# Retention in a hybrid S5/retention block: outputs with tokens on the rows, squares summed by ScalarE, products grouped by kind, loads issued one per step

## The reference, cut to what matters

```python
h   = rms_norm(x, norm_pre)                   # x: 1024 tokens x 2048
P   = h @ W_in                                # u_s | z_s | q | k | v | z_r | gl_s | gl_r
y_s = s5_mixer(u_s) * silu(z_s)
y_r = retention(q, k, v) * silu(z_r)          # 8 heads, q/k 64 wide, v 128 wide
m   = sigmoid(gl_s) * (y_s @ W_s) + sigmoid(gl_r) * (y_r @ W_r)
x   = x + rms_norm(m @ W_out, norm_post)

# retention, per head: rotary q, k; for each chunk of tokens
inner = ((q @ k.T) * decay) @ v
cross = (q * xi) @ state                      # the state before the chunk
state = state * chunk_decay + (k * zeta).T @ v
o     = inner + cross
o     = o * rsqrt(mean(o * o over the head's 128) + eps)
```

## Time and profile before

| | |
|---|---|
| median of 3 runs | 2518.59 us (2516.74 to 2531.87) |
| the profiled execution | 2524.69 us, span 2522.9 us |
| mean granted TensorE clock | 0.962 of 2.4 GHz |
| busy, PE / DVE / ACT / POOL | 2332.7 / 1853.4 / 1150.8 / 85.2 us |
| moved by DMA | 508.67 MB, mean 202 GB/s |

### The profile page before, as it was taken

How to read it: one execution, slowest core, us unless ns; L and a number is a source line. 1 busy time by engine, 2 the same in 40 slices (tenths; PEclk the granted TensorE clock), 3 DMA queues, 4 the chain that set the end, 5 groups by cost and what they waited for, 6 DMA issues and landing times.

```text
span 2522.9 us, 28579 instructions
## 1 busy us (share of the span) xinstructions
PE 2332.7 (92%) x10288; PEld 1892.8 (75%) x10288; DVE 1853.4 (73%) x2968; ACT 1150.8 (46%) x1814; POOL 85.2 (3%) x99
## 2 busy tenths in 40 slices
PE   7898999998999999988989996989999999799994
PEld 3676778787888888886777774767887777578883
DVE  6857992977898886626887754777678988767676
ACT  4343443456555554553445443334555444245552
POOL 0000000000000000000000000440000000000000
PEclk9999997999999999999999997899999999999997
DMA  7678456765456473769555767255656655855546
GB/s 271 217 232 253 133 171 217 262 209 197 120 183 211 145 244 111 256 199 296 180 184 157 280 187 255 68 201 175 212 196 210 224 185 180 291 200 189 182 130 254
DMA packets 287888, 508.67 MB, mean 202 GB/s; under 512 B 53201, under 2 KB 69601, under 8 KB 285569
## 3 DMA queue, kind: packets, MB, share of 16 engines
q1 hardware_dynamic: 242672, 430.00, 52.1%
q10 hardware_dynamic: 36560, 46.27, 5.3%
q0 software_dynamic: 8512, 30.56, 3.7%
HBM read 394.54 MB, written 112.20 MB: 201 GB/s over the span
## 4 chain that ended last, share of the span: by engine, by line
PE 67%; DVE 16%; DMA 6%; issue 4%; ACT 3%; SPq 3%; ACTq 1%; POOL 0%; DVEq 0%; POOLq 0%
PE psum L1473 16%; PE psum L1474 16%; PE psum L1475 16%; PE psum L1469 4%; PE psum L1471 4%; PE psum L1470 4%; DMA araw<-aops 4%; DVE a_lo L1085 3%; DVE b_lo L1087 3%; PE psum L1580 1%; PE psum L1578 1%; ACT a_hi L643 1%; DVE keep L1095 1%; PE psum L1529 1%; DMA aops<-work 1%
## 5 line engine op out<-in xcount | busy, mean ns | idle before, releaser
L643 ACT ACTIVATE a_hi<-araw 128x512 fp32r<-128x512 f32 x756 | 476.5, 630 | 1197.5 <-PE psum L1475 760.8
L1473 PE MATMUL psum<-a_hi,b_hi 128*128 128x512 f32 x2352 | 930.9, 396 | 97.8 <-DVE b_lo L1087 90.7
L1474 PE MATMUL psum<-a_hi,b_lo 128*128 128x512 f32 x2352 | 923.7, 393 | 0.0
L1475 PE MATMUL psum<-a_lo,b_hi 128*128 128x512 f32 x2352 | 922.8, 392 | 0.0
L1085 DVE TENSOR_TENSOR a_lo<-araw,a_hi 128x512 fp32r<-128x512 f32 x756 | 520.9, 689 | 535.5 <-ACT a_hi L643 534.1
L1473 PEld LDWEIGHTS psum<-a_hi,b_hi 128*128 128x128 f32 x2352 | 446.6, 190 | 213.5 <-DVE b_lo L1087 107.7
L1475 PEld LDWEIGHTS psum<-a_lo,b_hi 128*128 128x128 f32 x2352 | 446.5, 190 | 94.5
L1474 PEld LDWEIGHTS psum<-a_hi,b_lo 128*128 128x128 f32 x2352 | 446.8, 190 | 91.6
L1469 PE MATMUL psum<-b_hi,a_hi 128*128 128x512 f32 x672 | 268.4, 399 | 30.2 <-DVE b_lo L1087 29.6
L1087 DVE TENSOR_TENSOR b_lo<-bx,b_hi 128x512 fp32r<-128x512 f32 x432 | 295.5, 684 | 0.0
L653 ACT ACTIVATE b_hi<-bx 128x512 fp32r<-128x512 f32 x432 | 266.5, 617 | 0.5 <-DMA bx<-in_wstream 0.2
(11 more groups left out here) (147 smaller groups left out, 1618.8 us busy)
## 6 DMA issues: line engine op xcount, KB each, us to landing
araw<-aops SPq DMA_DIRECT2D x744, 256.0 KB, 2.7
bz<-in_wstream SPq DMA_DIRECT2D x216, 256.0 KB, 3.7
bx<-in_wstream SPq DMA_DIRECT2D x116, 256.0 KB, 4.7
aops<-work SPq DMA_DIRECT2D x28, 1024.0 KB, 5.7
spill<-keep ACTq DMA_DIRECT2D x28, 1024.0 KB, 5.8
by<-in_wstream SPq DMA_DIRECT2D x108, 256.0 KB, 5.5
work<-spill SPq DMA_DIRECT2D x20, 1024.0 KB, 7.6
aops<-work POOLq DMA_DIRECT2D x15, 1024.0 KB, 5.4
```

What stands on the lines that cost most here:

```text
L643: A.activation(a_hi[:, r, :], araw[:, s % A_RING, :], ACT.Copy).then_inc(head, 1)
L1473: T.matmul(bank, b_hi[:, r, cols], a_hi[:, r, :], start=first, stop=False, skip_group_check=on)
L1474: T.matmul(bank, b_lo[:, r, cols], a_hi[:, r, :], start=False, stop=False, skip_group_check=on)
L1475: done = T.matmul(bank, b_hi[:, r, cols], a_lo[:, r, :], start=False, stop=last, skip_group_check=on)
```

## The change

1. o is computed with tokens on the partitions: the decayed scores are the stationary operand and v the moving one. All 8 products with v come first, then the 8 with the state. The squares of a head then lie along the row: ACT sums them with its accumulator, 8 calls of 128 x 128 per block. Root and reciprocal are on 128 x 8. ACT scales half of the heads (4 calls of 128 x 128), DVE the other half, PE transposes all 8 back, and DVE multiplies by z_r from PSUM. The products with ones and GpSimd's arithmetic go. The last block makes no new state.
2. Block 0's scores are made before GGR0's step 53 and decayed at its step 55, in the side banks 6 and 7. PE enters retention without a wait for ACT, and waits for ACT's last evacuation only before the first transpose of k. The last block's transposes stand before GGR1's step 3, its gating at DVE's step 5.
3. The q and k loads are issued one per step at GGR0's steps 18 to 49, v in 8 parts at every fourth step from 20 to 48, the tables at step 17 behind the waits. `load_zr` moves to GpSimd's queue.
4. y_r is loaded back at GGR1's steps 16, 19, 22 and 25, and summed at 34 to 37.
5. `load_b11` no longer loads weight tiles 4 to 7 ahead of a group that has 4.

```diff
@@ SP @@
+            def load_qk(n):
+                part, a, par, two = n // 16, n // 4 % 4, n // 2 % 2, n % 2
...
+            def load_v(n):
+                sp.dma_start(v_row[:, n, :], vrows[n]).then_inc(qkv_loaded, 16)
...
-                        load_b11(g4 + 1, k4)
+                        if k4 < TILES[g4 + 1]:
+                            load_b11(g4 + 1, k4)
...
-                if g == GGR0 and at == 44:
+                if g == GGR0 and at == 17:
                     sp.wait_ge(ys_stored, 7 * 16)
                     for b in range(4):
                         sp.wait_ge(kept_stored[b], store_until(GQK, b))
-                    load_qkv()
-                    load_zr(0)
-                    load_zr(1)
-                if g == GGR1 and at == 4:
-                    for n in range(2, 8):
-                        load_zr(n)
-                if g == GGR1 and at == 8:
...
+                    load_tables()
+                if g == GGR0 and 18 <= at < 50:
+                    load_qk(at - 18)
+                if g == GGR0 and 20 <= at < 52 and at % 4 == 0:
+                    load_v((at - 20) // 4)
+                if g == GGR1 and at in (16, 19, 22, 25):
+                    n = (at - 16) // 3
...
@@ GpSimd @@
+            load_zr(0)
+            load_zr(1)
             for n in range(BLOCKS):
-                    pool.tensor_tensor(o_t[n % 2][:, par], o_t[n % 2][:, par], o_sq[:, par], ALU.mult).then_inc(o_scaled, 1)
...
                 pool.wait_ge(z_scaled, 2 * n + 2)
...
+                if n + 2 < BLOCKS:
+                    load_zr(n + 2)
@@ ACT, retain, per block n @@
+                        A.activation(o_n[:, par], psum[:, 4 + par, :].rearrange("p (a n) -> p a n", a=4), ACT.Copy
+                                     ).then_inc(o_copied, 1)
+                    for hd in range(HEADS):
+                        act.wait_ge(o_copied, 2 * n + hd // 4 + 1)
+                        A.activation(o_junk[:, 8 * (n % 2) + hd, :], o_n[:, hd // 4, hd % 4, :], ACT.Square,
+                                     accum_out=o_sum[:, n % 2, hd:hd + 1]).then_inc(o_squared, 1)
...
+                    A.activation(o_rstd[:, n % 2, :], o_sum[:, n % 2, :], ACT.Sqrt, scale=1.0 / V_HEAD, bias=eps_sb[:, 0:1]
+                                 ).then_inc(ostd_ready, 1)
+                    act.wait_ge(o_inverse, n + 1)
+                    for a in range(4):
+                        last = A.activation(o_n[:, 0, a, :], o_n[:, 0, a, :], ACT.Copy, scale=o_rstd[:, n % 2, a:a + 1])
+                    last.then_inc(o_scaled_act, 1)
@@ DVE @@
+            def next_state(n):
+                dve.wait_ge(kv_full, n + 1)
+                dve.wait_ge(o_full, 2 * n + 2)
...
+            def scale_o(n):
+                dve.wait_ge(ostd_ready, n + 1)
+                V.reciprocal(o_rstd[:, n % 2, :], o_rstd[:, n % 2, :]).then_inc(o_inverse, 1)
+                dve.wait_ge(o_inverse, n + 1)
+                V.tensor_tensor(o_t[n % 2][:, 1], o_t[n % 2][:, 1],
+                                o_rstd[:, n % 2, 4:8].unsqueeze(2).broadcast_to([P, 4, V_HEAD]), ALU.mult).then_inc(o_scaled_dve, 1)
+            def gate_o(n):
+                dve.wait_ge(o_turned, n + 1)
...
+                for par in range(2):
+                    V.tensor_tensor(yr_ring[:, n % 2, par::2, :], psum[:, 2 + par, :].rearrange("p (a n) -> p a n", a=4),
+                                    zr_ring[:, n % 2, par::2, :], ALU.mult).then_inc(z_scaled, 1)
+            def retain():
+                for n in range(BLOCKS):
+                    if n + 1 < BLOCKS:
+                        scale_q(n + 1)
+                        decay_scores(n + 1)
+                        if n == 0:
+                            scale_k(0)
+                        next_state(n)
+                        if n + 2 < BLOCKS:
+                            scale_k(n + 1)
                     if n:
+                        gate_o(n - 1)
+                    scale_o(n)
@@ PE, retain, per block n, and the step loop @@
+                    pe.wait_ge(scores_decayed, 2 * n + 2)
+                    if n:
+                        pe.wait_ge(o_copied, 2 * n)
+                            T.matmul(psum[:, 4 + par, 128 * a:128 * a + 128], s_dec[:, par, 128 * a:128 * a + 128],
+                                     v_row[:, n, V_HEAD * hd:V_HEAD * hd + V_HEAD], start=(a == 0), stop=False,
+                                     skip_group_check=True)
+                    if n == 0:
+                        pe.wait_ge(act_evac, 4 * GGR1)
+                        turn_k(0)
+                    pe.wait_ge(q_xi_ready, n + 1)
                     if n:
+                        pe.wait_ge(state_ready, 4 * n)
+                            last = T.matmul(psum[:, 4 + par, 128 * a:128 * a + 128], q_xi[rows, a, :], ret_state[rows, a, :],
+                                            start=False, stop=(a == 3), skip_group_check=True)
                     if n + 1 < BLOCKS:
                         scores(n + 1)
+                        pe.wait_ge(k_zeta_ready, n + 1)
...
+                    if n + 2 < BLOCKS:
+                        turn_k(n + 1)
+                    if n:
+                        turn_o(n - 1)
...
+                if s == BASE[GGR0] + 53:
+                    pe.wait_ge(dve_evac, 3 * GGR0 + 3)
+                    pe.wait_ge(qkv_loaded, 40 * 16)
+                    scores(0)
                 if s == BASE[GGR1]:
                     retain()
+                if s == BASE[GGR1] + 3:
+                    turn_o(BLOCKS - 1)
                 multiply(s)
```

More of the change, by code:

```diff
@@ L409, in load_zs, with load_tables @@
                              spill[1, i, 4 * c:4 * c + 4].rearrange("k p m -> p k m")).then_inc(zs_loaded[n % 2], 16)
[L411 to L427, removed]
+            def load_qk(n):
+                part, a, par, two = n // 16, n // 4 % 4, n // 2 % 2, n % 2
+                dst = k_t if part else q_t
+                row = 32 * (2 * (a % 2) + par)
+                src = spill[4, :, 4 * part + 2 * two + a // 2, row:row + 32, :].rearrange("i p m -> p i m")
+                rows = slice(64 * par + 32 * two, 64 * par + 32 * two + 32)
+                sp.dma_start(dst[rows, a, :].rearrange("p (i m) -> p i m", i=2), src).then_inc(qkv_loaded, 16)
+            def load_v(n):
+                sp.dma_start(v_row[:, n, :], vrows[n]).then_inc(qkv_loaded, 16)
+            def load_tables():
                 sp.dma_start(area(16384, 1024), dmat).then_inc(tables_loaded, 16)
@@ L666, in free @@
                     act.wait_ge(yr_stored[1], 4 * 32)
+                if g == GGR1 and b == 1:
+                    act.wait_ge(o_turned, 8)
                 if stored(g - 1):
@@ new lines, in gate_o @@
+            def gate_o(n):
+                dve.wait_ge(o_turned, n + 1)
+                dve.wait_ge(zr_loaded[n % 2], 16 * (n // 2 + 1))
+                if n >= 2:
+                    dve.wait_ge(yr_stored[n % 2], 32 * (n // 2))
+                else:
+                    dve.wait_ge(kept_stored[0], store_until(GGR0, 0))
+                for par in range(2):
+                    V.tensor_tensor(yr_ring[:, n % 2, par::2, :], psum[:, 2 + par, :].rearrange("p (a n) -> p a n", a=4),
+                                    zr_ring[:, n % 2, par::2, :], ALU.mult).then_inc(z_scaled, 1)
@@ L1532, in outputs, with scores @@
                 pe.wait_ge(gelu_done, 8)
+            def scores(n):
+                tok = slice(BLOCK * n, BLOCK * n + BLOCK)
+                if n:
+                    pe.wait_ge(scores_decayed, 2 * n)
+                for a in range(4):
+                    for par in range(2):
+                        rows = slice(64 * par, 64 * par + 64)
+                        last = T.matmul(psum[:, 6 + par, 128 * a:128 * a + 128], k_t[rows, a, tok], q_t[rows, a, tok],
+                                        start=True, stop=True)
+                        if a == 3:
+                            last.then_inc(scores_full, 1)
@@ new lines, in turn_k, with turn_o @@
+            def turn_k(n):
+                tok = slice(BLOCK * n, BLOCK * n + BLOCK)
+                if n:
+                    pe.wait_ge(k_zeta_ready, n)
+                for a in range(4):
+                    last = T.transpose(psum[:, 0, 128 * a:128 * a + 128], k_t[:, a, tok], eye_sb[:, :])
+                last.then_inc(k_turned, 1)
+            def turn_o(n):
+                pe.wait_ge(o_scaled_act, n + 1)
+                pe.wait_ge(o_scaled_dve, n + 1)
+                if n:
+                    pe.wait_ge(z_scaled, 2 * n)
+                for par in range(2):
+                    for a in range(4):
+                        last = T.transpose(psum[:, 2 + par, 128 * a:128 * a + 128], o_t[n % 2][:, par, a, :], eye_sb[:, :])
+                last.then_inc(o_turned, 1)
@@ L1589, in retain @@
+                                last.then_inc(o_full, 1)
                     if n + 1 < BLOCKS:
                         scores(n + 1)
[L1591 to L1596 removed]
```

(7 more changed lines are left out.)

181 lines of the change are left out of this document (68 added, 113 removed).

## The result

| | before | after |
|---|---|---|
| median of 4 runs each, same chip | 2519.27 us (2516.74 to 2531.87) | 2448.05 us (2445.5 to 2449.89) |
| ratio, 95% interval | | 0.9707 (0.9673 to 0.9741) |
| the traced execution, its span | 2524.69, 2522.9 us | 2446.9, 2445.1 us |
| mean granted TensorE clock | 0.962 | 0.971 |
| busy PE / DVE / ACT / POOL | 2332.7 / 1853.4 / 1150.8 / 85.2 us | 2279.0 / 1814.6 / 1160.3 / 50.3 us |

The forecast was 2449.

What follows compares the result with a forecast made beforehand. PE was taken as the bound, through its holes, low-clock stretches and retention blocks. Terms led by -43.1 (retention), -25.4 (loads) and -8.0 (y_r) summed to -69.7 us, giving 2449 against 2518.59; range 2436 to 2462, probability 0.64.

Steps and rivals of the forecast that it cites:

- what would show it: Signs listed beforehand on PE's holes, product runs, block spacing, clock and loop resumption that would show the forecast right or wrong.
- A block, 7.1: Retention: each steady block takes 7.1 us, set by ACT (PE 6.8, DVE 6.1 to 6.5); range 6.5 to 8.5.
- The start: Start of retention: v(0) starts at once, o(0) ends at 4.9 us, with holes of 1.2 and 2.0 us.
- The 2 us for the clock: Retention: 2 us added in case the two early holes bring one more short stretch at half rate.
- Loads: GGR0: spreading the q, k and v loads over the steps removes the lump's idle time and slow step, -25.4 us.
- Step 17, +2.5: GGR0: SP waits about 7 us for y_s stores, delaying step 18's tile; 0 to 7 us, 2.5 taken.
- Sums, +3.8: GGR1 steps 34 to 37: moved y_r sums crowd DVE, 4.8 us of stall against 1.0; +3.8 (0 to 7).
- y_r, last transposes: GGR1: four spread y_r loads, -8.0 us; last transposes before step 3, +1.0, while a 1.6 us hole goes.
- The clock rival: Retention: clock stays low as transposes count less as PE activity; 2495 at full price, 2458 with one stretch; chance 0.12.
- ACT as the bound: Rival in retention: squares at 0.82 us and scalings at 0.63 keep blocks at 11 us; +28, 2477; chance 0.12.
- The loads giving their gain back: Rival in GGR0: spread loads make tiles late in a third of 34 steps, returning 22 us; 2471; chance 0.07.
- SP held at each issue: Rival in GGR0 steps 18 to 49: each of 40 loads holds SP 5.5 us; +63 in all, 2582; chance 0.02.

Runs made afterwards that it cites:

- e8: The changed kernel with each of ACT's 8 squares per block computed twice; 2461.79 us.
- e6: The changed kernel with the y_s wait at step 19, tables at 24, q/k loads from 21, and y_r sums at steps 37, 39, 41, 44; 2441.19 us.
- e1: The changed kernel with its loads issued in one go at GGR0's step 44 again, z_r back on SP's queue; 2470.88 us.
- e5: The changed kernel itself, unchanged, rerun on the chip of e6; 2446.89 us.
- e2: The kernel before with only the q, k, v and table loads spread over GGR0's steps 17 to 49; 2504.09 us.
- e12: The same kernel as e11, run again for a second trace; 2470.74 us.
- e10: The changed kernel with y_r loaded in one go at GGR1's step 8 and summed early, as before; 2454.52 us.
- e9: The changed kernel without the head start: block 0's scores and decays back at the start of retention; 2451.09 us.
- e3: The changed kernel with o's v and state products alternating again instead of grouped; 2492.09 us.
- e4: The kernel before with only its products of o grouped by kind; 2507.27 us.
- e7: e4 with DVE's reciprocals on 8 columns instead of 512, leaving out part of the normalisation; 2489.53 us.
- e11: The changed kernel with v and state products alternating from block 2 on, blocks 0 and 1 as changed; 2474.17 us.

## Why the prediction was right, and by how much it was off

**The bound.** Right: the time came from PE's holes and from PE's block, in the places named. Of the points under "what would show it", no idle above 2 us in GGR0's steps 40 to 52, o's products in two runs of 1.88 and 1.00, no hole of over 5 us at step 18 or at steps 35 to 38: all as written. Two came out below what was given: new state products 6.26 us apart for 7.0 to 7.3, and 51 us to the resumed loop for 58 to 60.

**A block, 7.1: mis-sized, 6.26.** The failed step is the price of a square on ACT. I added the accumulator's 0.185 to a call of 0.32; the rows show 0.30 and 0.19, overlapping, 0.29 from start to start. That is 1.7 us less a block, and ACT, which the forecast had as the bound, has room (e8). PE's 6.8 was 6.26 because no waits between kinds came (0.3 were kept) and 64-row products take 1.00, not 1.09, from start to start. The DVE sum, 6.1 to 6.5, was too high as well: 5.64 of work and 0.62 of waiting. It added records of 0.68, while calls start 0.60 apart. It also took the product for q at 0.68 in the kernel before, where it has 1.15 in steady blocks (L1243), and is 0.69 now. Over the chain of blocks 6.26 for 7.1 makes 5.5 us.

**The start.** Right: o(0) ended 4.9 us in (forecast 4.9), o(1) 12.3 (12.7). The holes are 1.28 and 1.97 us for the 1.2 and 2.0 named. The 2 us for the clock were not needed in this trace; in e6's, with the same holes, 1.6 of them were. They belong in the range, since holes of one size brought a low stretch in some traces (e1, e6) and none in others (after, e5).

**Loads.** -25.6 for -25.4; e1 confirms it from the other side. In the kernel before the same edit took the same 25.6 us out of steps 44 to 47 and gave 18.9 in all (e2): the term carries over, what comes with it does not.

**Step 17, +2.5: mis-sized, +4.8.** The mechanism and the 7 us of standing were right (7.3). The landing was not worked out: the tile for step 18, issued at 1431.0, landed 7.3 us later, in a stretch where DMA was 1.04 busy. Standing 7.3, tables 1.3, landing 7.3, less the 10.9 of the four slots, is 5.0. The rows of before had landings of 10.5 us, for 1 MB each, in the same stretch; I should have used them for the tile too. The term varies from trace to trace: in e5's, the same kernel, it is +3.3, and in those of e8 to e12, which leave these steps as they are, +5.1 to +5.7.

**Sums, +3.8: mis-sized, +0.9.** The stall is 3.1 where 4.8 were forecast, and the old place lost 2.2 in two steps where I had read one row of 1.0.

**y_r, last transposes.** -8.1 for -8.0, and -1.0 for -0.6; e10 shows y_r from the other side. No run takes the weight tiles of point 5 alone; the 0 given to them fits, but is not shown.

**The clock rival: excluded for this mix of work.** 12 transposes in 6.26 us, and 1.00 over all 50.66 us of retention, in this trace and over the blocks of e9. The Trainium skill's page "TensorE: Matmul & The Clock Gate" (Part 4, PE-mode transpose) has it that a transpose does not count as PE activity the way a product does. At 1.4 us of transposes in 6.26 no run here shows a loss from it. What the clock did follow is the order of the products behind a hole (e3 against e9, e4 against before), and that stood in my rows: 19.5 us at 0.50 in the alternating first block. I took them for the price of the hole.

**The other rivals.** ACT as the bound: excluded, with 0.95 us of room. The loads giving their gain back: excluded, 30.00 of 30.00 us busy in GGR0. SP held at each issue: excluded, 0.43 us an issue beside the tiles.

**Why 2449 fits so closely.** Partly by compensation. On the traces the forecast was 8 us short (-69.7 for -77.8): 5.5 for the blocks, 2 for the clock and 2.9 for the sums one way, 2.3 for step 17 the other. The trace of before lay 5.4 us above its median and the one after 1.2 below, which took 6.6 of these back on the medians. With e5 the change is 74.5 us, between the two.

## What to carry to other kernels

Count small products by the starts of a row in the trace that has them in the order in question: here the same 16 cost 6.6 us in alternation and 2.9 grouped, which in the changed kernel was worth more than any transfer moved (44 us for 23), and 15.8 in the kernel before, where another wait took most of it. Where a queue is made to wait, the price is the standing plus the landing of what it issues next, less what its slots cover; moving the wait two steps later and the tables seven was worth 3.1 to 4.7 us in this case, depending on which of the two traces of the changed kernel e6 is held against. And a forecast made against one traced execution carries that execution's distance from the median, here 5 to 6 us of 70.

## What the runs showed of the hardware

- **Alternating fp32 products of 128 and 64 rows** start every 0.42 us, grouped every 0.235 and 0.125. The Trainium skill's page "TensorEngine Tiling (Array Packing)" (Key Properties) says that a change of the tiling mode drains TensorE. The rows agree: 3.7 us more for 16 such products, 0.23 each. Not all of it need be the change of mode. Grouped, the state products take the two halves of the rows in turn, 0.125 us apart, and in alternation they do not; no run here separates the two.
- **The low clock lasts longer under alternation.** Behind a hole of 3.1 to 3.3 us it lasted 6.8 us with grouped products (e4, e7, e9) and 17.1 to 34.1 with alternating ones (before, e2, e3), with PE busy for nearly all of it. At full clock six blocks of alternation left it at 1.00 in both traces of e11 and e12; in e2 a stretch of 10.2 us at 0.50 began under alternation without a hole, unexplained.
- **A small ACT call with an accumulator** costs 0.29 us from start to start at 128 x 128.
- **DVE's product of two SBUF tiles**, 128 x 512, takes 1.03 us in e7, where GpSimd multiplies beside it, and 0.69 in the changed kernel, where GpSimd only issues DMAs. No run tests GpSimd's part in it alone.
